# Retention heads: VectorE places all blocks of k, ScalarE all blocks of v

## The chip, the cores and the metric

The kernel runs on one core of one Trainium2 chip. The time is device microseconds (us) of that core, the median of the runs shown. One further execution was profiled, and all rows come from that one.

## The reference, cut to what matters

One step of a two-layer trunk over 320 tokens: 256 of a prompt, 64 of a second group that continues a stored state. Layer 0 projects its input once, to 8 retention heads and a pooling mixer. Layer 1 is an mLSTM mixer. A gated feed-forward block follows each. The change touches the retention heads alone:

```
q, k = rotary(q, pos), rotary(k, pos) * 128 ** -0.5
s      = (q . k) * decay                      # l x m, causal
intra  = s . v                                # sum over tokens m
inter  = (q . S) * q_decay                    # the stored state, second group only
S_new  = gamma ** L * S + (k * k_decay)^T . v  # sum over tokens
ret    = head_rms(intra + inter) * silu(gate)
```

The projections come out with features on the partitions. Both sums over tokens need k and v with tokens on the partitions, so each head turns two arrays of 128 features x 320 tokens.

## The kernel before, in words

**Weights.** All weight matrices are cut into 768 units of 128 x 1024 numbers and pass through a ring of four slots. SyncE (SP) loads a unit (`load`, its issue is L394). ScalarE (ACT) rounds it into `w_hi` (`split`, L909). VectorE (DVE) subtracts to get `w_lo` (`split`, L1323). TensorE (PE) multiplies it (`unit`, L560, 24 matmuls in the retention stage). ScalarE may split unit u only when TensorE has used unit u-4 to the end (it waits for `unit_used` at u-3), and SP may load unit u only when VectorE has split unit u-4. TensorE waits for `lo_ready` before each unit.

**Heads.** A head takes eight units, j = 0 to 7. The first four make q and k in two banks of PSUM, the last four v and the gate. Work that belongs to a head but not to its projection is written out by hand at fixed places j in the next head's units, separately on each engine; each engine takes its own list in order. Head 0's tail and head 1's projection lie in a part of their own ahead of the loop (units 8 to 15). The loops `Fori(0, HEADS - 2)` do the projections of heads 2 to 7 beside the tails of heads 1 to 6. The tail of head 7 runs beside the pooling units.

**Order on VectorE,** for projection h+1 beside tail h, each time after the split of that place: j=0 v and gate scaled by `rt` (L1431, L1432) and v turned by 32 x 32 blocks (L1434, `v_turned`); j=1 half of v placed (L1439); j=2 gate (L1443); j=3 states copied out (L1448, L1449); j=4 rotary on q and k (L1380 to L1389); j=5 k weighted and turned (L1416, L1418, `k_turned`) and half of k placed (L1425); j=6 normalise (L1455, L1456, L1458); j=7 the low part of the result (L1462) and the scores weighted by decay (L1408 to L1411, `ret_intra`). In the part of head 0 the order differs: v of head 0 is turned at j=1, k of head 0 placed at j=1, v of head 0 placed and its scores weighted at j=2, and k of head 1 is turned at j=5 and placed at j=6.

**Order on ScalarE:** j=1 half of v placed (L934) and then the tanh of the gate with its table load (L927); j=4 two copies out of PSUM (L947, L948); j=5 square root (L952); j=6 half of k placed (L942); j=7 high part of the result (L958). In the part of head 0, k is placed at j=1 and v at j=2.

**What "placing" is.** A turn by 32 x 32 blocks leaves each block turned but in its old place. Placing moves block (s, f) from partitions 32f to partitions 32s. One instruction does one pair (s, f) for all token tiles: 32 partitions by 96 for s = 0, 1 and by 64 for s = 2, 3. An array has 16 of them. Before, ScalarE does s = 0, 2 and VectorE s = 1, 3 of both arrays.

**TensorE.** `ret_sums` (L636) stands after the unit of j = 2 of the next head (in the part of head 0, after j = 4). It waits for all four placing semaphores, for `ret_intra` and for the state's load (`ret_s0_loaded`). The units behind it are queued behind that wait. SP issues the state's load (L446) after the store of the previous head's states, behind the eighth load of a head.

Of the kernel before, what the change touches and what calls it, by code (L numbers as in the profile page):

```python
# [10 lines left out]
ACT = mybir.ActivationFunctionType  # L11
# [130 lines left out]
def trunk_kernel(nc, x_in, weights, w_pool_in, cols_in, consts_in, ret_tables_in, ret_state_in, ml_state_in,  # L142
                 y_out, ret_out, pool_out, c_out, m_out, conv_out, ffn_out, m_scratch):
    with ExitStack() as ctx:
# [3 lines left out]
        def sem(name):  # L148
            return ctx.enter_context(nc.semaphore(name))
# [16 lines left out]
        def piece(width, restart=False):  # L166
            if restart:
                used[0] = 0
            at = used[0]
            used[0] += width  # L170
            assert used[0] <= WORK, used
            return work[:, at:at + width]
# [14 lines left out]
        k_tok, v_tok = piece(3 * P), piece(3 * P)  # L187
# [60 lines left out]
        def token_blocks(at):  # L248

            return work[:, at:at + 3 * P].rearrange("p (n s a) -> p n s a", n=3, s=4)  # L250

        k_blocks, v_blocks = token_blocks(k_blocks_at), token_blocks(v_blocks_at)

        def turned_block(turned, s, f):

            return turned[f * 32:(f + 1) * 32, 0:3 - s // 2, s, :]

        def token_rows(tok, s, f):

            return tok.rearrange("p (n c) -> p n c", n=3)[s * 32:(s + 1) * 32, 0:3 - s // 2, f * 32:(f + 1) * 32]  # L260
# [51 lines left out]
        def bank(b, m):  # L312
            return gb[:, 2 * b + m, 0:T]
# [15 lines left out]
        def sems(text):  # L329
            return [sem(name) for name in text.split()]  # L330
# [15 lines left out]
            "first_squares first_sum last_added last_squares z_ready rt_half")  # L346
        dve_step, = sems("dve_step")

        qk_raw, qk_ready, ret_intra, v_tok_ready, ret_state, mix_ready = sems(
            "qk_raw qk_ready ret_intra v_tok_ready ret_state mix_ready")  # L350
        ret_scores, ret_summed, ret_sq_sum = sems("ret_scores ret_summed ret_sq_sum")
        v_turned, v_tok_act, k_turned, k_tok_ready, k_tok_act, gate_ready = sems(
            "v_turned v_tok_act k_turned k_tok_ready k_tok_act gate_ready")
        gate_tanh, ret_sq, ret_std, mix_hi = sems("gate_tanh ret_sq ret_std mix_hi")
        b_ready, = sems("b_ready")
        pooled_ready, pool_summed, pool_hi = sems("pooled_ready pool_summed pool_hi")
# [191 lines left out]
        def _(pe):  # L548
# [86 lines left out]
            def small(out, lhs, rhs, start=True, stop=True):  # L635
                return nc.tensor.matmul(out, lhs, rhs, start=start, stop=stop)  # L636
# [18 lines left out]
                small(ab[:, 2, SEQ + P:SC], k_pad[:, SEQ:3 * P], q_t[:, SEQ:T]).then_inc(ret_scores, 1)  # L655

            def ret_sums(h):
                pe.wait_ge(v_tok_ready, h + 1)
                pe.wait_ge(v_tok_act, h + 1)
                pe.wait_ge(k_tok_ready, h + 1)  # L660
                pe.wait_ge(k_tok_act, h + 1)
                pe.wait_ge(ret_intra, h + 1)
                pe.wait_ge(ret_s0_loaded, h * 16 + 16)
                small(ab[:, 3, 0:SEQ], v_tok[:, 0:P], s_t[:, 0:SEQ], stop=False)
                small(ab[:, 3, P:SEQ], v_tok[:, P:2 * P], s_t[:, SEQ:SEQ + P], start=False)
                small(ab[:, 3, SEQ:T], v_tok[:, 2 * P:3 * P], s_t[:, SEQ + P:SC], stop=False)
                small(ab[:, 3, SEQ:T], ret_s0, q_dec, start=False)
                small(ab[:, 0, 0:P], k_tok[:, 0:P], v_tok[:, 0:P], stop=False)
                small(ab[:, 0, 0:P], k_tok[:, P:2 * P], v_tok[:, P:2 * P], start=False)
                small(ab[:, 0, P:2 * P], k_tok[:, 2 * P:3 * P], v_tok[:, 2 * P:3 * P])\  # L670
                    .then_inc(ret_summed, 1)
# [81 lines left out]
            for p in range(POOL_GROUPS):  # L753
                for kg in range(4):
                    j = 4 * p + kg
# [133 lines left out]
            for m in range(2):  # L889
# [5 lines left out]
                last = small(ab[:, 0, 0:T], ones, sq_last[:, m * T:(m + 1) * T], start=False, stop=m == 1)  # L895
# [4 lines left out]
        def _(act):  # L900
            def split(u):

                if not u.exists:
                    return
                act.wait_ge(raw_loaded[u.slot], u.turn(16, 16))
                if u.i is not None or u.first >= RING:
                    act.wait_ge(unit_used, u.number(1 - RING))
                at = u.slot * UW
                nc.scalar.activation(w_hi[:, at:at + UW], raw[:, at:at + UW], ACT.Copy).then_inc(hi_ready, 1)  # L909
# [19 lines left out]
            def ret_place_v(h):  # L929

                act.wait_ge(v_turned, h + 1)
                for s in (0, 2):
                    for f in range(4):
                        last = nc.scalar.activation(token_rows(v_tok, s, f), turned_block(v_blocks, s, f), ACT.Copy)  # L934
                last.then_inc(v_tok_act, 1)

            def ret_place_k(h):

                act.wait_ge(k_turned, h + 1)
                for s in (0, 2):  # L940
                    for f in range(4):
                        last = nc.scalar.activation(token_rows(k_tok, s, f), turned_block(k_blocks, s, f), ACT.Copy)  # L942
                last.then_inc(k_tok_act, 1)

            def ret_squares(h):
                act.wait_ge(ret_summed, h + 1)
# [56 lines left out]
            for j in range(8):  # L1003
                split(Unit(8 + AHEAD + j))
                if j == 0:
                    act.wait_ge(con_loaded, 16)
                    norm(0)
                if j == 1:
                    ret_place_k(0)
                if j == 2:  # L1010
                    ret_place_v(0)
                    ret_gate(0)
                if j == 5:
                    ret_squares(0)
                if j == 6:
                    ret_std_of(0)
                    ret_place_k(1)
                if j == 7:
                    ret_mix(0)
            with act.Fori(0, HEADS - 2) as i:  # L1020
                for j in range(8):
                    split(Unit(16 + AHEAD + j, i, 8))
                    ret_tail(i + 1, j)
                    if j == 6:
                        ret_place_k(i + 2)
            for j in range(16):
                split(Unit(U_POOL + AHEAD + j))
                ret_tail(HEADS - 1, j)
# [276 lines left out]
        def _(dve):  # L1305
            step = Count(dve_step)
            V = nc.vector
# [31 lines left out]
            def used(u_last):  # L1339

                dve.wait_ge(unit_used, u_last)
# [78 lines left out]
            def ret_place_k(h):  # L1420

                dve.wait_ge(k_turned, h + 1)
                for s in (1, 3):
                    for f in range(4):
                        last = V.tensor_copy(token_rows(k_tok, s, f), turned_block(k_blocks, s, f))  # L1425
                last.then_inc(k_tok_ready, 1)

            def ret_tail(h, j, stored=True):
                if j == 0:
                    used(h * 8 + 8)  # L1430
                    V.tensor_tensor(v_t, bank(1, 0), rt[:], ALU.mult)  # L1431
                    V.tensor_tensor(z_g, bank(1, 1), rt[:], ALU.mult).then_inc(pair_taken, 1)  # L1432
                    dve.wait_ge(pair_taken, h * 2 + 2)
                    V.transpose(o_rs, v_t).then_inc(v_turned, 1)  # L1434
                if j == 1:
                    dve.wait_ge(v_turned, h + 1)
                    for s in (1, 3):
                        for f in range(4):
                            last = V.tensor_copy(token_rows(v_tok, s, f), turned_block(v_blocks, s, f))  # L1439
                    last.then_inc(v_tok_ready, 1)  # L1440
                if j == 2:
                    dve.wait_ge(gate_tanh, h + 1)
                    V.scalar_tensor_tensor(gate, tanh_g, 1.0, z_g, ALU.add, ALU.mult).then_inc(gate_ready, 1)  # L1443
                if j == 3:
                    dve.wait_ge(ret_summed, h + 1)
                    if stored:
                        dve.wait_ge(ret_stored, h * 16)
                    V.tensor_copy(s_new[:, 0:RET_DV], ab[:, 0, 0:P])  # L1448
                    V.scalar_tensor_tensor(s_new[:, RET_DV:2 * RET_DV], ret_s0,  # L1449
                                           con[:, bass.ds(h + CON["gamma_l"], 1)], ab[:, 0, P:2 * P],  # L1450
                                           ALU.mult, ALU.add).then_inc(ret_state, 1)
                if j == 6:
                    dve.wait_ge(gate_ready, h + 1)
                    dve.wait_ge(ret_std, h + 1)
                    step.inc(V.tensor_tensor(mix, mix, gate, ALU.mult))  # L1455
                    step.inc(V.reciprocal(o_rs, o_std))  # L1456
                    own()
                    V.tensor_tensor(mix, mix, o_rs, ALU.mult).then_inc(mix_ready, 1)  # L1458
                if j == 7:
                    dve.wait_ge(mix_ready, h + 1)  # L1460
                    dve.wait_ge(mix_hi, h + 1)
                    V.tensor_tensor(low(b, h), mix, high(b, h).bitcast(F32), ALU.subtract)\  # L1462
                        .then_inc(b_ready, 1)
# [857 lines left out]
```

## Time and profile before

| | us |
|---|---|
| median of 3 runs (2769.45 to 2769.46) | 2769.45 |
| the profiled execution | 2768.36 |
| its span | 2766.5 |
| PE busy | 2745.8 (99%) |
| PEld busy | 2495.7 (90%) |
| DVE busy | 1949.3 (70%) |
| ACT busy | 1453.2 (53%) |

The span is the part that the profile covers; the execution's own time is 1.86 us longer. PE is TensorE's matmuls, PEld its weight loads, which overlap the matmuls. The busy shares are of the span. The clock granted to TensorE was 0.999 of full over the run.

### The profile page before, as it was taken

To read this page: it belongs to the slowest core of one execution; us is meant where nothing else is said; L and a number is where in the kernel's file an instruction comes from. 1 tells how busy PE (TensorE), PEld (TensorE's weight loads), DVE (VectorE), ACT (ScalarE), POOL (GpSimd) and SP (SyncE) were. 2 spreads that over 40 slices of the span, in tenths; PEclk is the share of its full clock that TensorE was granted. 3 is DMA by queue.
4 is the path that set the end of the run, shared out by engine and by line. 5 is a ranking of instruction groups with operands and counts; after the bars stand their busy time and mean duration, and the time that the engine had idled before them with its cause. 6 is when DMAs were issued, how large, how long until landed. Compare 5 with 4: busy or idle time off the path is not lost.

```text
span 2766.5 us, 44056 instructions
## 1 busy us (share of the span) xinstructions
PE 2745.8 (99%) x15341; PEld 2495.7 (90%) x15341; DVE 1949.3 (70%) x3202; ACT 1453.2 (53%) x2441; POOL 160.3 (6%) x134
## 2 busy tenths in 40 slices
PE   9999999999999999999999999999999999999998
PEld 8999988888888888888999999888888888888887
DVE  8877677676567665668887778667675667655776
ACT  6555345665345543555555566546654455535554
POOL 0000032000000000002300000330000000000004
PEclk9999999999999999999999999999999999999999
DMA  6444345454545454544444444444444444444443
GB/s 241 153 154 152 125 137 165 143 165 140 167 142 164 143 165 141 165 143 148 161 149 147 153 147 154 140 146 152 157 148 160 146 159 148 155 160 147 152 149 128
DMA packets 120999, 422.64 MB, mean 153 GB/s; under 512 B 13704, under 2 KB 18320, under 8 KB 120720
## 3 DMA queue, kind: packets, MB, share of 16 engines
q1 hardware_dynamic: 120704, 420.41, 46.3%
q8 instruction: 120, 1.97, 0.3%
q14 instruction: 31, 0.25, 0.0%
q10 hardware_dynamic: 144, 0.01, 0.0%
HBM read 414.22 MB, written 6.14 MB: 152 GB/s over the span
## 4 chain that ended last, share of the span: by engine, by line
PE 94%; DVE 3%; ACT 1%; issue 1%; DMA 1%; SPq 0%; DVEq 0%; ACTq 0%
PE gb L600 38%; PE gb L610 25%; PE gb L560 18%; PE ab L570 10%; PE ab L636 3%; DVE w_lo L1323 1%; ACT w_hi L909 1%; DMA raw<-in_weights 1%; ACT work L1039 0%; DVE rt L1336 0%; DVE work L1494 0%; DVE work L2160 0%; DVE work L1892 0%; DVE work L1547 0%; ACT work L999 0%
## 5 line engine op out<-in xcount | busy, mean ns | idle before, releaser
L1323 DVE TENSOR_TENSOR w_lo<-raw,w_hi 128x1024 fp32r<-128x1024 f32 x766 | 951.2, 1254 | 512.2 <-ACT w_hi L909 507.2
L909 ACT ACTIVATE w_hi<-raw 128x1024 fp32r<-128x1024 f32 x768 | 809.0, 1058 | 873.1 <-PE gb L610 416.0
L600 PE MATMUL gb<-a,w_hi 128*128 128x512 f32 x2816 | 684.0, 390 | 0.0
L560 PE MATMUL gb<-a,w_hi 128*128 128x320 f32 x2784 | 619.4, 311 | 3.6 <-DVE a L1330 2.1
L600 PEld LDWEIGHTS gb<-a,w_hi 128*128 128x128 f32 x2816 | 525.0, 188 | 105.4
L560 PEld LDWEIGHTS gb<-a,w_hi 128*128 128x128 f32 x2784 | 464.8, 188 | 6.4 <-DVE a L1330 2.4
L600 PE MATMUL gb<-b,w_hi 128*128 128x512 f32 x1920 | 464.8, 390 | 0.0
L560 PE MATMUL gb<-a,w_lo 128*128 128x320 f32 x1392 | 430.2, 309 | 0.0
L610 PE MATMUL gb<-a,w_lo 128*128 128x320 f32 x2816 | 426.9, 309 | 0.0
L610 PEld LDWEIGHTS gb<-a,w_lo 128*128 128x128 f32 x2816 | 419.8, 188 | 6.8
L600 PEld LDWEIGHTS gb<-b,w_hi 128*128 128x128 f32 x1920 | 358.0, 188 | 71.8
L1039 ACT ACTIVATE work<-work 32x128 f32<-32x128 f32 x960 | 295.7, 308 | 206.5 <-DVE work L1347 195.7
L610 PE MATMUL gb<-b,w_lo 128*128 128x320 f32 x1920 | 292.5, 309 | 0.0
L610 PEld LDWEIGHTS gb<-b,w_lo 128*128 128x128 f32 x1920 | 286.8, 188 | 5.4
L560 PEld LDWEIGHTS gb<-a,w_lo 128*128 128x128 f32 x1392 | 261.3, 188 | 0.0
L520 POOL TENSOR_TENSOR sq_one<-x 128x320 f32 x60 | 69.8, 1163 | 2573.1 <-DVE x L1371 2562.5
L570 PE MATMUL ab<-w_hi,a 128*128 128x512 f32 x704 | 188.6, 390 | 0.6 <-ACT w_hi L909 0.6
L570 PEld LDWEIGHTS ab<-w_hi,a 128*128 128x128 f32 x704 | 131.8, 188 | 29.0 <-ACT w_hi L909 1.9
L570 PE MATMUL ab<-w_hi,b 128*128 128x512 f32 x480 | 128.8, 390 | 0.2 <-ACT w_hi L909 0.2
L570 PEld LDWEIGHTS ab<-w_hi,b 128*128 128x128 f32 x480 | 89.5, 188 | 19.3 <-DVE b L1715 0.7
L1659 DVE TENSOR_TENSOR work<-gb,rt 128x384 f32<-128x384 f32 x44 | 24.6, 559 | 105.0 <-PE gb L600 105.0
L1369 DVE TENSOR_TENSOR x<-gb,x 128x640 f32 (+1 forms) x63 | 52.0, 825 | 64.5 <-PE gb L600 53.1
(216 smaller groups left out, 1662.9 us busy)
## 6 DMA issues: line engine op xcount, KB each, us to landing
raw<-in_weights SPq DMA_DIRECT2D x768, 512.0 KB, 3.4
work<-in_ret_tables SPq DMA_DIRECT2D x8, 320.0 KB, 3.7
out_c<-work SPq DMA_DIRECT2D x8, 257.0 KB, 5.1
x<-in_x SPq DMA_DIRECT2D x3, 640.0 KB, 8.9
work<-m_scratch SPq DMA_DIRECT2D x8, 192.0 KB, 4.8
out_y<-work SPq DMA_DIRECT2D x3, 480.0 KB, 3.5
work<-in_ml_state SPq DMA_DIRECT2D x8, 128.5 KB, 4.7
raw<-in_weights SPq DMA_DIRECT2D x4, 256.0 KB, 4.9
```

The costliest lines, as they stand in the source:

```text
L520: step.inc(nc.gpsimd.tensor_tensor(sq_one[:], tile(x, t), tile(x, t), ALU.mult))
L560: last = nc.tensor.matmul(bank(b, m), w[:, at:at + P], v, start=kg == k == n == 0, stop=kg == groups - 1 and k == UK - 1 and n == 2)
L570: last = nc.tensor.matmul(out, act[:, t:t + P], w[:, :, k, :], start=q == k == 0, stop=q == quads - 1 and k == UK - 1)
L600: last = nc.tensor.matmul(gb[:, 2 * p + m, :], w_hi[:, at:at + P], act[:, t:t + 512], start=q == k == 0, stop=final and low_first and k == ...
L610: last = nc.tensor.matmul(bank(p, m), w_lo[:, at:at + P], act[:, t:t + T], start=False, stop=final and not low_first and k == UK - 1)
L636: return nc.tensor.matmul(out, lhs, rhs, start=start, stop=stop)
L909: nc.scalar.activation(w_hi[:, at:at + UW], raw[:, at:at + UW], ACT.Copy).then_inc(hi_ready, 1)
L1039: last = nc.scalar.activation(left_t_blocks[feats * 32:(feats + 1) * 32, :, tokens, :], left_blocks[tokens * 32:(tokens + 1) * 32, :, feat ...
L1323: V.tensor_tensor(w_lo[:, at:at + UW], raw[:, at:at + UW], w_hi[:, at:at + UW].bitcast(F32), ALU.subtract).then_inc(lo_ready, 1)
L1369: step.inc(V.tensor_tensor(two(tiles(x, p * 2)), banks(b), two(tiles(x, p * 2)), ALU.add))
L1659: V.tensor_tensor(two(low_gate)[:, :, 0:WIDE_LO], lows_of(0), r[:, :, 0:WIDE_LO], ALU.mult)
```

## The change

The numbers of instructions, their shapes and their sources stay; who issues them and when changes. VectorE's `ret_place_k` now does all four s, 16 copies where it did 8; ScalarE's is gone. ScalarE's `ret_place_v` does all four s, 16 copies where it did 8; VectorE's placing of v at j = 1 is gone. The semaphores `v_tok_ready` and `k_tok_act` go, and with them two of TensorE's waits.

```diff
             def ret_sums(h):
-                pe.wait_ge(v_tok_ready, h + 1)
                 pe.wait_ge(v_tok_act, h + 1)
                 pe.wait_ge(k_tok_ready, h + 1)
-                pe.wait_ge(k_tok_act, h + 1)
                 pe.wait_ge(ret_intra, h + 1)
...
             def ret_place_v(h):      # ScalarE
                 act.wait_ge(v_turned, h + 1)
-                for s in (0, 2):
+                for s in range(4):
                     for f in range(4):
                         last = nc.scalar.activation(token_rows(v_tok, s, f), turned_block(v_blocks, s, f), ACT.Copy)
                 last.then_inc(v_tok_act, 1)
-
-            def ret_place_k(h):
-
-                act.wait_ge(k_turned, h + 1)
-                for s in (0, 2):
-                    for f in range(4):
-                        last = nc.scalar.activation(token_rows(k_tok, s, f), turned_block(k_blocks, s, f), ACT.Copy)
-                last.then_inc(k_tok_act, 1)
...
-                if j == 1:
-                    ret_place_k(0)
...
                     ret_std_of(0)
-                    ret_place_k(1)
...
                     ret_tail(i + 1, j)
-                    if j == 6:
-                        ret_place_k(i + 2)
...
             def ret_place_k(h):      # VectorE
                 dve.wait_ge(k_turned, h + 1)
-                for s in (1, 3):
+                for s in range(4):
                     for f in range(4):
                         last = V.tensor_copy(token_rows(k_tok, s, f), turned_block(k_blocks, s, f))
                 last.then_inc(k_tok_ready, 1)
...
-                if j == 1:
-                    dve.wait_ge(v_turned, h + 1)
-                    for s in (1, 3):
-                        for f in range(4):
-                            last = V.tensor_copy(token_rows(v_tok, s, f), turned_block(v_blocks, s, f))
-                    last.then_inc(v_tok_ready, 1)
```

## Rows read from the trace of the kernel before

**Rows 1.** The page: busy time and share of each engine; chain that ended last.

```profile
PE 2745.8 (99%) x15341; PEld 2495.7 (90%) x15341; DVE 1949.3 (70%) x3202; ACT 1453.2 (53%) x2441; POOL 160.3 (6%) x134
...
PE 94%; DVE 3%; ACT 1%; issue 1%; DMA 1%; SPq 0%; DVEq 0%; ACTq 0%
```

**Rows 2.** Waits of PE: releaser, us in total, times, longest.

```profile
PE ab L636 <- DVE b L1462: 0.6, 1, 0.6
...
PE ab L636 <- DVE work L1411: 0.4, 1, 0.4
```

**Rows 3.** Timeline of DVE, head 0: start, duration (both us), line, count.

```profile
50.91 0.51 DVE L1434 STREAM_TRANSPOSE work<-work 128x320 f32<-128x320 f32 x1
51.45 1.71 DVE L1425 COPY work<-work 32x96 f32<-32x96 f32 x8
...
56.87 0.21 DVE L1411 TENSOR_TENSOR work<-work 128x64 f32<-128x64 f32 x1
57.20 1.23 DVE L1323 TENSOR_TENSOR w_lo<-raw,w_hi 128x1024 fp32r<-128x1024 f32 x1
```

**Rows 4.** Timeline of ACT, head 0, the second placing and what follows.

```profile
52.22 2.21 ACT L934 ACTIVATE work<-work 32x96 f32<-32x96 f32 x8
...
56.12 1.05 ACT L909 ACTIVATE w_hi<-raw 128x1024 fp32r<-128x1024 f32 x1
```

**Rows 5.** Timeline of PEld (weight loads), the sums of head 0.

```profile
57.30 0.84 PEld L636 LDWEIGHTS ab<-work 128*128 128x128 f32 x5 [0.64 <-issue]
```

**Rows 6.** Timeline of DVE, from k of head 1 to v of head 1.

```profile
67.61 1.72 DVE L1425 COPY work<-work 32x96 f32<-32x96 f32 x8
...
71.94 0.49 DVE L1458 TENSOR_TENSOR work<-work 128x320 f32<-128x320 f32 x1
...
76.74 0.51 DVE L1434 STREAM_TRANSPOSE work<-work 128x320 f32<-128x320 f32 x1
```

**Rows 7.** Timeline of ACT beside it.

```profile
72.47 0.47 ACT L958 ACTIVATE b<-work 128x320 fp32r<-128x320 f32 x1 [2.65 <-DVE work L1458]
...
77.28 2.22 ACT L934 ACTIVATE work<-work 32x96 f32<-32x96 f32 x8 [1.34 <-DVE work L1434]
...
81.19 1.99 ACT L909 ACTIVATE w_hi<-raw 128x1024 fp32r<-128x1024 f32 x2
87.21 1.06 ACT L909 ACTIVATE w_hi<-raw 128x1024 fp32r<-128x1024 f32 x1 [4.03 <-PE gb L560]
```

**Rows 8.** Timeline of PE, the sums of head 1.

```profile
81.72 0.59 PE L636 MATMUL ab<-work 128*128 128x256 f32 x2
```

**Rows 9.** Timeline of SPq, the state's load for head 1; its time to landing.

```profile
78.00 0.34 SPq L446 DMA_DIRECT2D work<-in_ret_state  x1
...
DMA to landing us min/median/max: 3.2/3.2/3.2
```

**Rows 10.** Timeline of DVE in the loop, up to v of head 3.

```profile
132.51 0.49 DVE L1458 TENSOR_TENSOR work<-work 128x320 f32<-128x320 f32 x1
...
135.26 1.22 DVE L1323 TENSOR_TENSOR w_lo<-raw,w_hi 128x1024 fp32r<-128x1024 f32 x1
...
137.31 0.51 DVE L1434 STREAM_TRANSPOSE work<-work 128x320 f32<-128x320 f32 x1
```

**Rows 11.** Timeline of ACT in the loop, the same head.

```profile
133.13 0.47 ACT L958 ACTIVATE b<-work 128x320 f32 x1 [2.42 <-DVE work L1458]
134.05 1.06 ACT L909 ACTIVATE w_hi<-raw 128x1024 fp32r<-128x1024 f32 x1 [0.45 <-PE gb L560]
137.57 1.06 ACT L909 ACTIVATE w_hi<-raw 128x1024 fp32r<-128x1024 f32 x1 [2.46 <-PE gb L560]
138.54 2.21 ACT L934 ACTIVATE work<-work 32x96 f32<-32x96 f32 x8
```

**Rows 12.** Timeline of PEld and of PE, the sums of head 3.

```profile
144.27 0.88 PEld L636 LDWEIGHTS ab<-work 128*128 128x128 f32 x5
...
144.41 0.81 PE L636 MATMUL ab<-work 128*128 128x256 f32 x4
```

More of the change, by code:

```diff
@@ L347, in trunk_kernel @@
         dve_step, = sems("dve_step")
-        qk_raw, qk_ready, ret_intra, v_tok_ready, ret_state, mix_ready = sems(
-            "qk_raw qk_ready ret_intra v_tok_ready ret_state mix_ready")
+        qk_raw, qk_ready, ret_intra, ret_state, mix_ready = sems(
+            "qk_raw qk_ready ret_intra ret_state mix_ready")
         ret_scores, ret_summed, ret_sq_sum = sems("ret_scores ret_summed ret_sq_sum")
-        v_turned, v_tok_act, k_turned, k_tok_ready, k_tok_act, gate_ready = sems(
-            "v_turned v_tok_act k_turned k_tok_ready k_tok_act gate_ready")
+        v_turned, v_tok_act, k_turned, k_tok_ready, gate_ready = sems(
+            "v_turned v_tok_act k_turned k_tok_ready gate_ready")
         gate_tanh, ret_sq, ret_std, mix_hi = sems("gate_tanh ret_sq ret_std mix_hi")
```

## The prediction, made before the changed kernel was run

> **What bounds the kernel now.** I read the page's busy shares and chain first: TensorE is busy for 99% of the span and makes 94% of the chain that ended last [rows 1]. No engine beside it can make the kernel faster by more than the little that TensorE stands idle; any stall of TensorE that the change adds is paid in full, unless a later wait takes it back. So the second view is who TensorE waits for. Two entries touch the retention heads: 0.4 us for the decay weighting of head 0 (L1411) and 0.6 us for the last low part of the heads, L1462 [rows 2]. No placing releases it anywhere. The third view is therefore the timeline around `ret_sums`, engine by engine: how long before TensorE arrives are k and v in place? I did this for head 0, head 1 and a head of the loop, since the three have different neighbours.
>
> **What the change is, in instructions.** Per array and head, eight copies on VectorE last 1.71 to 1.72 us [rows 3, 6], eight on ScalarE 2.21 to 2.22 [rows 4, 7, 11]. In all VectorE loses and gains 64 copies, ScalarE too, so total busy time hardly moves. What moves is place. On VectorE, 1.72 us goes from behind v's turn to ahead of it. On ScalarE, 2.2 us that lay beside VectorE's half now stands in line behind it: v is placed 4.43 us after its turn (2.21 for the first eight, 2.22 from start to start for the second), where it took ScalarE 2.21 and VectorE about as long.
>
> **Head 0.** v's turn starts at 50.91 and lasts 0.51 [rows 3]. ScalarE, now without k, starts at 51.45 and ends 4.43 later, at 55.88. VectorE places k from 51.45 to 54.92, then splits and weights; it did 8 + split + 8 before and does 16 + split now, so L1411 still starts at 56.87 and ends at 57.08 [rows 3]. TensorE's weight load came at 57.30, 0.22 later [rows 5]. v is ready 1.2 us before that: cost 0, and the 0.4 us wait stays as well. But ScalarE's tanh and splits follow its placing. The split of unit 14 started 1.69 after eight copies had ended (54.43 to 56.12 [rows 4]); now it starts at 55.88 + 1.69 = 57.57, lasts 1.06, and VectorE, which waits for it, starts its own at 58.66 instead of 57.20 [rows 3]. VectorE runs on without a gap from there to k of head 1, so everything up to 67.61 [rows 6] comes 1.46 late. Nothing that TensorE needs in this stretch is late.
>
> **Head 1.** k of head 1 costs VectorE 1.72 more at j = 6, and it stays without a gap: 1.46 + 1.72 = 3.18 late. v's turn, 76.74 before [rows 6], starts at 79.92 and ends at 80.43. ScalarE starts as before 0.03 later (77.25 to 77.28 [rows 6, 7]), at 80.46; its high part and two splits come in time, since its row at 72.47 moves with L1458 [rows 6, 7] to 75.65 and two splits of about 1 us follow. It ends at 80.46 + 4.43 = 84.89. TensorE is there much earlier: the sums' first matmul was at 81.72 [rows 8], its weight load 0.14 ahead as in the loop [rows 12], at 81.58. With the 0.22 from release to weight load it starts at 85.11. **Stall: 85.11 - 81.58 = 3.5 us.** All units of TensorE behind `ret_sums` wait with it. For the price of passing a release, the bounds are 0.03 (VectorE to ScalarE, rows 6 and 7) and 0.22 (rows 3 and 5): I take the second, which is TensorE's own. Both ends give 3.3 to 3.5.
>
> **Is it given back?** The lateness of ScalarE and VectorE against TensorE goes at the next place where they wait for it: ScalarE stood idle for 4.03 us before its split at 87.21 [rows 7]. After the change the pair of splits ahead of it starts at 84.89 + 1.69 = 86.58 instead of 81.19, and TensorE has moved by 3.5, so against TensorE ScalarE is 1.9 later, within those 4.03. TensorE itself has no gap in the heads that it could shorten. The 0.6 us for L1462 [rows 2] comes from work on VectorE that starts at a unit's end, so it travels with TensorE and stays.
>
> **Heads 2 to 7,** all alike, by head 3. VectorE comes to the loop's k as before, since both helpers have caught up. Sixteen copies make it 1.72 late; v's turn moves from 137.31 [rows 10] to 139.03 and ends at 139.54. ScalarE's high part moves from 133.13 with L1458 [rows 10, 11] to 134.85 and its next split (at most 0.45 later, as it waited before) to 135.3, done at 136.4; VectorE needs it at 135.26 + 1.72 = 136.98 [rows 10]. The split at 137.57 [rows 11] stays, so ScalarE is free at 138.6, starts at 139.57 and ends at 144.00. TensorE's weight load stands at 144.27 [rows 12]. Ready at 144.03 to 144.22, by the two bounds: a slack of 0.05 to 0.24 us, where ScalarE's half had 3.5 to spare. Cost 0, but barely, six times; if the estimate is wrong by 0.2 us, each head pays about 0.1.
>
> **Transfers.** The loads of weights wait for VectorE's splits, which come up to 3.2 us late once; ScalarE's splits are later still. The state of head 1 matters more: its issue at 78.00 stands behind the load released by such a split. 78.00 + 3.18 + 3.2 to landing [rows 9] = 84.4, half a microsecond ahead of v. Hidden, and late next if v were faster. The waits removed from TensorE cost nothing that the trace shows.
>
> **The page against the row.** ScalarE's eight copies take 2.21 us, 0.28 each, beginning to end, no overlap between neighbours [rows 4, 11]. The Trainium skill, page "ScalarE: Activation LUTs", section "What ACT_TABLE_LOAD costs", gives an ACTIVATE with immediate scale 186 ns + 0.833 ns per element and says that back-to-back ones overlap by about 93 ns. By that sixteen would take an estimated 8 x 0.173 + 8 x 0.146 = 2.55 us; head 0 would then make nothing late, v of head 1 would be there at 77.28 + 1.72 + 2.55 + 0.22 = 81.8, the state's load at 82.9 would be last, and the stall 1.3 us. The trace disagrees with the page for these 32-partition copies, and decides.
>
> **The sum.** 2768.36 of the profiled execution + 3.5 = 2771.9. The median of the runs is 1.09 higher than that execution, so 2769.45 + 3.5 = 2772.95, some 0.13% slower. What a measurement of this kernel can tell from no change is about 0.2%, 5.5 us: by that bound the forecast is "same", with a sign.
>
> **Rivals.**
> 1. *Every head stalls.* The slack of 0.05 to 0.24 in the loop is gone because a copy for s = 1, 3 is dearer on ScalarE, or because ScalarE's high part, now close to its loop's end, delays the split and with it v's turn. For: six heads with almost no slack. Against: the shapes are the same, and the split has 0.6 us of its own slack. Price: 3.5 + 6 x (0.1 to 0.5) = 4.1 to 6.5, say 2774.2. Beyond 0.2% only where a head loses 0.34 or more. Chance 0.14.
> 2. *Not slower.* v of head 1 comes in time, because VectorE isn't late: it would need ScalarE's split of unit 14 to come in time and the second half of v to be placed within 1.1 us of v's turn; or the wait for L1411 falls, worth 0.4. It decides from where v's turn of head 1 ends before 81.58 - 0.22 - 4.43 = 76.9, which is even earlier than the 77.25 of now. So a stall of 0.3 comes with no lateness at all. Price: -0.4 to +0.3, 2769.4. Chance 0.08.
> 3. *The state's load is last.* If it is stretched by the weights' loads beside it, by 1 us, it lands at 85.4 and the stall is 4.2: 2773.6. Chance 0.08.
> 4. *Sixteen copies cost ScalarE less than twice eight,* because neighbours overlap in a longer run. The nearest faster rows are VectorE's own, 2 x 1.72 = 3.44 [rows 6]. Then v of head 0 ends at 54.89, VectorE is 0.47 late and not 1.46, v of head 1 is turned at 79.44 and ready at 79.47 + 3.44 + 0.22 = 83.1; the state's load at 78.00 + 2.19 + 3.2 = 83.4 is last. Price 1.8: 2771.3. Against: the eight show no sign of it. Chance 0.06. The page named above is this rival's, with a still smaller stall.
>
> The forecast has 0.64. **Range:** it takes in rivals 3 and 4 and most of 1, and the release bounds: 2770.5 to 2775.6. Slower by over 0.2% is the far part of rival 1 and what I don't see, 0.07. Faster by over 0.2% would need 5.5 us out of TensorE's idle time, of which two named waits of the heads make 1.0 us: 0.02. Within 0.2%: 0.91.
>
> **What would show it.** Right: a new entry among TensorE's waits, L636 released by ScalarE's placing (L934 of now), once, 3.4 to 3.6 us long, near 81.7; L934 in runs of 16 lasting 4.4 us; v's turn of head 1 near 79.9; ScalarE's idle time for k gone; the sums of the loop's heads 31.3 us apart with gaps under 0.1. Wrong: no gap at 81.7, or the releaser is a DMA, or six gaps of equal size. The forecast is wrong as a whole if the span grows by less than 2 us or more than 5.

## The result, and the profile after

| | kernel before | changed kernel |
|---|---|---|
| median of 9 runs, us | 2769.38 (2768.57 to 2769.93) | 2777.71 (2774.62 to 2780.66) |
| profiled execution, us | 2768.36 | 2780.66 |
| its span, us | 2766.5 | 2778.9 |

The ratio is 1.0031 (95% interval 1.0022 to 1.0039): the change costs 8.3 us. Forecast were 3.5 us, a time of 2773.0 and a range up to 2775.6. The direction was right; the size was not, and the result lies outside the range. The changed kernel also scatters over 6 us where the kernel before scatters over 1.4, and its profiled execution is the slowest of the nine. What is read from its trace explains 12.4 us of span, more than the median lost. Line numbers have moved: in the changed kernel L932 is ScalarE's placing of v, L907 its split and L925 the tanh; L1308 is VectorE's split, L1403 the turn of k, L1410 its placing and L1419 the turn of v.

The page, the lines that answer to [rows 1]: busy time of each engine, and the chain that ended last.

```profile
PE 2749.6 (99%) x15341; PEld 2498.0 (90%) x15341; DVE 1947.5 (70%) x3202; ACT 1452.8 (52%) x2441; POOL 160.2 (6%) x134
...
PE 87%; DVE 6%; ACT 3%; DMA 2%; issue 1%; SPq 0%; DVEq 0%; ACTq 0%
```

Busy times hardly move, as forecast. But the chain leaves TensorE far more often, and it now has a share of DMA twice as large. The waits of PE (us in total, times, longest), which answer to [rows 2]:

```profile
PE ab L636 <- ACT work L932: 9.5, 7, 3.2
```

One such entry was forecast, once, 3.4 to 3.6 us long. It is there seven times. (The longest is 3.2 us by the matmuls and 3.51 us by the weight loads, which were to start first; from here on gaps are those of the weight loads.) Where in the heads it stands is seen in the timeline of PEld, the weight loads with which `ret_sums` begins (start, duration, and in brackets the gap before and its releaser). They answer to [rows 5, 8, 12]; shown are heads 0, 1, 2 and 7, and the gaps of heads 3 to 6 are 1.48, 1.45, 1.33 and 1.21:

```profile
58.26 1.85 PEld L636 LDWEIGHTS ab<-work 128*128 128x128 f32 x14 [0.35 <-issue]
...
86.08 1.85 PEld L636 LDWEIGHTS ab<-work 128*128 128x128 f32 x14 [3.51 <-ACT work L932]
...
118.59 1.85 PEld L636 LDWEIGHTS ab<-work 128*128 128x128 f32 x14 [1.17 <-ACT work L932]
...
281.99 1.85 PEld L636 LDWEIGHTS ab<-work 128*128 128x128 f32 x14 [1.17 <-ACT work L932]
```

The sums of head 1 in the kernel before, which had no gap:

```profile
81.57 1.89 PEld L636 LDWEIGHTS ab<-work 128*128 128x128 f32 x14
```

From there to the sums of head 3 at 144.27 [rows 12] are 62.70 us: before, the sums of the loop's heads stood 31.35 us apart. From 86.08 to 281.99 are 195.91 us, against 6 x 31.35 = 188.10: the six heads of the loop lose 7.81. The account of the 12.4 us:

- up to the sums of head 0: 58.26 - 57.30 [rows 5] = 0.96. This isn't put down to the change. At 41 us, ahead of the first placed block, TensorE is already 1.25 us late (42.42 against 41.17); in the nine traces of the experiments it is 0.2 to 1.2 us late there. The granted clock averages 0.66 between 15 and 20 us, against 1.00 in the trace of before; but it is 0.66 in the repeat of the changed kernel too (experiment 5), whose sums start at 57.29.
- head 1: 86.08 - 81.57 (before) - 0.96 = 3.55, the stall that was forecast.
- heads 2 to 7: 7.81, forecast at nothing.
- what is left is 0.1: behind the heads the two kernels run alike.

**Who makes the loop's heads late.** The waits of DVE between 40 and 330 us have an entry that the kernel before doesn't have:

```profile
DVE work L1401 <- DMA work<-in_ret_tables: 8.7, 6, 1.6
```

L1401 is the first line of `ret_turn_k`, which multiplies k by the head's decay. It waits for the load of the decay table, once in each of six heads. The timeline of DVE for one of them, from the split ahead of k's turn to the turn of v:

```profile
97.95 1.22 DVE L1308 TENSOR_TENSOR w_lo<-raw,w_hi 128x1024 fp32r<-128x1024 f32 x1
100.50 0.49 DVE L1401 TENSOR_TENSOR work<-work 128x320 f32<-128x320 f32 x1 [1.33 <-DMA work<-in_ret_tables]
...
113.54 0.51 DVE L1419 STREAM_TRANSPOSE work<-work 128x320 f32<-128x320 f32 x1
```

k's turn is 1.33 late by the table, the sixteen copies add their 1.72, and v's turn follows. ScalarE starts on v at 114.09, ends at 118.55, and TensorE starts at 118.59, 1.17 late.

**Why the table is late.** SP issues it behind the fourth load of the head's weights, and each load of weights waits until VectorE's split has set its buffer free. First the issues of SPq for the table of head 2 in the kernel before (start, duration), and the time of each to landing (last number, in the same order):

```profile
83.66 0.33 SPq L394 DMA_DIRECT2D raw<-in_weights  x1
85.20 0.33 SPq L394 DMA_DIRECT2D raw<-in_weights  x1
89.69 0.33 SPq L394 DMA_DIRECT2D raw<-in_weights  x1
90.22 0.33 SPq L441 DMA_DIRECT2D work<-in_ret_tables  x1
```
```profile
raw<-in_weights SPq DMA_DIRECT2D x1, 512.0 KB, 3.3
raw<-in_weights SPq DMA_DIRECT2D x1, 512.0 KB, 4.0
raw<-in_weights SPq DMA_DIRECT2D x1, 512.0 KB, 3.4
work<-in_ret_tables SPq DMA_DIRECT2D x1, 320.0 KB, 3.6
```

The same for the changed kernel:

```profile
90.19 0.33 SPq L394 DMA_DIRECT2D raw<-in_weights  x1
91.73 0.33 SPq L394 DMA_DIRECT2D raw<-in_weights  x1
94.16 0.33 SPq L394 DMA_DIRECT2D raw<-in_weights  x1
94.68 0.33 SPq L441 DMA_DIRECT2D work<-in_ret_tables  x1
```
```profile
raw<-in_weights SPq DMA_DIRECT2D x1, 512.0 KB, 3.3
raw<-in_weights SPq DMA_DIRECT2D x1, 512.0 KB, 4.5
raw<-in_weights SPq DMA_DIRECT2D x1, 512.0 KB, 5.5
work<-in_ret_tables SPq DMA_DIRECT2D x1, 320.0 KB, 5.8
```

The first two loads are released 6.5 us later than before, the third and the table only 4.5 later. What was spread over 6.6 us is now issued within 4.5. The table lands 5.8 us after its issue, at 100.5, which is where L1401 starts. The cause of the late release is ScalarE's timeline:

```profile
81.58 4.45 ACT L932 ACTIVATE work<-work 32x96 f32<-32x96 f32 x16 [2.44 <-DVE work L1419]
86.04 1.28 ACT L925 ACT_TABLE_LOAD   x1
87.34 0.47 ACT L925 ACTIVATE work<-work 128x320 f32<-128x320 f32 x1
87.72 1.99 ACT L907 ACTIVATE w_hi<-raw 128x1024 fp32r<-128x1024 f32 x2
```

Its next two splits stand behind sixteen copies, a table load and the tanh, so they start at 87.72 instead of 81.19 [rows 7]. VectorE's splits and SP's loads follow them. TensorE, meanwhile, has only moved by 4.5.

### The profile page after: what moved, and what is told of

It reads as the page before. It is cut to its first block, busy times and chain, and to the rows that moved or that the text cites. A ratio compares the mean times of both kernels' runs of the same rounds, so it can differ in the third digit from the quotient of the medians.

```text
span 2778.9 us, 44042 instructions
## 1 busy us (share of the span) xinstructions
PE 2749.6 (99%) x15341; PEld 2498.0 (90%) x15341; DVE 1947.5 (70%) x3202; ACT 1452.8 (52%) x2441; POOL 160.2 (6%) x134
## 4 chain that ended last, share of the span: by engine, by line
PE 87%; DVE 6%; ACT 3%; DMA 2%; issue 1%; SPq 0%; DVEq 0%; ACTq 0%
PE gb L600 38%; PE gb L610 24%; PE gb L560 13%; PE ab L570 10%; PE ab L636 2%; DVE w_lo L1308 2%; DMA work<-in_ret_tables 1%; ACT work L932 1%; ACT w_hi L907 1%; DVE work L1410 1%; DVE work L1435 1%; ACT work L1024 0%; DMA raw<-in_weights 0%; DVE rt L1321 0%; DVE work L1419 0%
## 5 line engine op out<-in xcount | busy, mean ns | idle before, releaser
L1308 DVE TENSOR_TENSOR w_lo<-raw,w_hi 128x1024 fp32r<-128x1024 f32 x766 | 950.5, 1253 | 516.3 <-ACT w_hi L907 511.5
L907 ACT ACTIVATE w_hi<-raw 128x1024 fp32r<-128x1024 f32 x768 | 807.8, 1058 | 849.1 <-PE gb L610 416.0
```

The costliest lines, as they stand in the source:

```text
L1308: V.tensor_tensor(w_lo[:, at:at + UW], raw[:, at:at + UW], w_hi[:, at:at + UW].bitcast(F32), ALU.subtract).then_inc(lo_ready, 1)
```

## The experiments

All were timed in five rounds beside runs of the kernel before on the same chip. The ratios are to that kernel.

**1. The table's load early.** The changed kernel, with the decay table issued behind the first load of weights instead of the fourth.

```diff
-                for j in range(4):
-                    load(Unit(8 + j, h, 8))
+                load(Unit(8, h, 8))
                 sp.wait_ge(ret_intra, h)
                 sp.dma_start(ret_table, head_row(ret_tables_in, h)).then_inc(ret_table_loaded, 16)
-                for j in range(4, 8):
+                for j in range(1, 8):
                     load(Unit(8 + j, h, 8))
```

> The changed kernel, with the load of a head's decay table issued by SP behind the first of the head's eight weight loads and not behind the fourth. Theory (table): in heads 2 to 7 VectorE waits for this table before it can weight and turn k, because ScalarE's long placing of v makes the two weight loads ahead of it late, so that three loads and the table go out within 4.5 us and the table lands in 5.8 instead of 3.6. Then the table is there in time, VectorE's wait for it goes, the six stalls of 1.2 to 1.5 us fall to 0.1 or less, and only head 1's 3.5 stays: 2769.4 + 3.5 = 2772.9, with less spread from run to run than the changed kernel (2774.6 to 2780.7). Rival (copies): v placed by ScalarE alone is too slow in every head whatever the table does; six stalls stay near 1.3 and the time near 2777.7.

Measured: 2773.98 (2773.19 to 2775.15, 11 runs) against 2769.07 (2768.36 to 2770.70, 33 runs), ratio 1.0019 (1.0010 to 1.0028). VectorE doesn't wait for the table any more. PEld's timeline, the sums of heads 1, 2 and 7:

```profile
85.18 3.35 PEld L635 LDWEIGHTS ab<-work 128*128 128x128 f32 x14 [3.54 <-ACT work L931]
...
118.14 1.89 PEld L635 LDWEIGHTS ab<-work 128*128 128x128 f32 x14
...
274.87 1.89 PEld L635 LDWEIGHTS ab<-work 128*128 128x128 f32 x14
```

Head 1's stall is as it was; from head 2 to head 7 are 156.73 us, which is 5 x 31.35 to within 0.02, and no gap is left. So the table's late landing is needed for the loop's stalls, and the slack of 0.05 to 0.24 us that was forecast without it is enough. Measured it is 0.24: ScalarE's copies for head 3 end at 149.24, and the weight load starts at 149.48. The run is 1.1 us above the expectation, and one reason is in the first row: fourteen loads in 3.35 us where they took 1.85, and 32.96 us to the next sums instead of 31.35. The window just behind the stall in this kernel (the stretch; its length; busy time of PE, PEld, DVE, ACT and POOL; the granted clock; DMA share; GB/s):

```profile
86.00:87.00 1.00, 1.00 (x6) 0.94 (x5) 0.00 (x0) 0.99 (x3) 0.00 (x0) 0.50 0.01 5
```

In the stall the granted clock was 1.00. Behind it TensorE runs at 0.50, its 1.2 GHz level, and between 88.5 and 90.0 us the mean is back at 0.91. That makes the stall dearer by 32.96 - 31.35 = 1.6 us.

**2. Half of the change: ScalarE all of v,** k in halves as before. The edit is to the kernel before; VectorE's placing of v is gone.

```diff
             def ret_place_v(h):
...
-                for s in (0, 2):
+                for s in range(4):
```

> Half of the change: ScalarE places all of v, k stays half on each engine. Theory (table): ScalarE's splits behind the long placing are as late as in the changed kernel, so VectorE still waits 1.3 to 1.6 us for the table in heads 2 to 7, but VectorE has not the 1.7 us of further copies, v's turn is only about 1.5 late and the sums of heads 2 to 7 stall by 0.3 or less. Head 0: ScalarE places k, then all of v, its split of unit 14 starts at 58.3 instead of 56.1, VectorE is 2.2 late; the weighting comes early, so the old 0.4 us wait of head 0 goes. Head 1: v ready at 84.2 against 81.2, stall 3.0, net +2.6: 2772.0. Rival (copies): the loop's six heads stall by over 1 us here too, 2779.

Measured: 2774.23 (2771.97 to 2777.47, 11 runs), ratio 1.0020 (1.0011 to 1.0029). The forecast of six waits for the table was a miss:

```profile
DVE work L1415 <- DMA work<-in_ret_tables: 1.6, 2, 1.1
```
```profile
85.27 1.85 PEld L636 LDWEIGHTS ab<-work 128*128 128x128 f32 x14 [3.42 <-ACT work L933]
...
116.57 1.89 PEld L636 LDWEIGHTS ab<-work 128*128 128x128 f32 x14
```

The table comes late twice, and then on time: its median landing is 4.0 us, against 5.9 in the changed kernel. The two waits are for head 1, 0.48 us, and for head 2, 1.12. The first is part of head 1's gap, which was forecast at 3.0 and is 3.42. 31.30 us lie between the sums of heads 1 and 2, so the second cost nothing: VectorE, which has only eight copies of k, has 1.7 us more in hand. Moving v alone makes the stall of head 1 but not those of the loop. Its profiled span is 2771.3, 4.8 over that of before, and up to the last sums it had lost 3.65. The other 1.1 us come far behind the heads, in layer 1: two gaps of the weight loads, 0.41 us before 1572.19 and 0.59 before 1666.01, and among the waits of PE an entry that the kernel before doesn't have, for VectorE's L1897 (0.5 us, 2 times). Why VectorE is late there no run shows.

**3. The other half: VectorE all of k,** v in halves. ScalarE's placing of k is gone, as in the changed kernel.

```diff
             def ret_place_k(h):
...
-                for s in (1, 3):
+                for s in range(4):
```

> The other half of the change: VectorE places all of k, v stays half on each engine. Theory (table): ScalarE's splits are on time, the table lands in 3.6 to 3.7 us and VectorE does not wait for it; the loop's six heads have no stall, since v's second half is done by VectorE at 142.4 of 144.3. Head 0 pays: 16 copies of k and 8 of v stand ahead of the weighting, which is 1.7 late: stall 1.7 more. Head 1: VectorE 3.4 late, last copies ready at 83.8 against 83.3: 0.5. Sum +2.2: 2771.6. Rival (copies): no stall in the loop either, so only the table rows tell.

Measured: 2772.61 (2770.67 to 2773.15, 11 runs), ratio 1.0012 (1.0002 to 1.0021). Head 0's weighting is late by VectorE's longer line, as expected: 

```profile
60.10 2.56 PEld L636 LDWEIGHTS ab<-work 128*128 128x128 f32 x14 [2.22 <-issue]
...
86.24 1.85 PEld L636 LDWEIGHTS ab<-work 128*128 128x128 f32 x14 [0.26 <-issue]
```
```profile
62.00:63.00 1.00, 1.00 (x6) 1.00 (x6) 0.55 (x2) 0.01 (x1) 0.00 (x0) 0.50 0.77 225
```

The gap of 2.22 is 1.6 over the 0.64 of before, forecast 1.7. The window shows a granted clock of 0.50 here too, behind the gap. From these sums to the next are 26.14 us, against 24.27 before, of which 0.26 is a gap: the other 1.6 is the clock, more than the 1.0 us that the median lies over the 2771.6 expected. The loop has no stall and no wait for the table. By experiments 2 and 3, neither half makes the loop stall; only both together do.

**4. The table early, and ScalarE's split of unit 14 ahead of placing v of head 0.**

```diff
             for j in range(8):
-                split(Unit(8 + AHEAD + j))
+                if j != 3:
+                    split(Unit(8 + AHEAD + j))
...
                 if j == 2:
+                    split(Unit(8 + AHEAD + 3))
                     ret_place_v(0)
```

> As the table moved forward, and in the part of head 0 ScalarE splits unit 14 ahead of placing v of head 0 instead of behind the tanh. My account of head 1's 3.5 us is 1.5 of lateness from that split, 1.7 from the eight further copies of k and 0.3 from the second half of v. If it holds, the stall of head 1 falls to 2.0 and the time to 2769.4 + 2.0 = 2771.4. Rival: the state's load of head 1, half a microsecond behind v, is what ends the wait; it comes 1.5 earlier too, so then also about 2.0, but released by a DMA. If the split has no part in it, 3.5 stays and the time is as with the table moved alone.

Measured: 2770.84 (2770.10 to 2773.04, 11 runs), ratio 1.0007 (0.9998 to 1.0016).

```profile
83.62 1.85 PEld L635 LDWEIGHTS ab<-work 128*128 128x128 f32 x14 [1.98 <-ACT work L931]
```

The 1.46 us by which the prediction held VectorE late out of head 0 are worth 3.54 - 1.98 = 1.56 of head 1's stall. The medians of experiments 1 and 4 differ by more, 3.1 us: here the clock doesn't fall behind the stall (31.31 us to the next sums), and in experiment 1's trace that cost 1.6. What is left is 2770.84 - 2769.07 = 1.8 us of the change's 8.3, with an interval that takes in no change, though each engine still places a whole array.

**5. The changed kernel once more,** for its scatter.

> The changed kernel itself once more, on the chip of these runs, for a second profile and for its spread. The table account: the loop's six stalls come with a table that lands in 4.5 to 6 us behind two or three weight loads that are still in flight; landings differ from run to run, so the six stalls differ, between 0.3 and 1.5 us each, and the time spreads over some 6 us (2774.6 to 2780.7 so far) where the kernel before spreads over 2. Rival (copies): the stalls are set by the engines' instruction times, which repeat to 0.1 us, and would be alike in both profiles; the spread is then without a cause in the heads.

Measured: 2778.76 (2778.49 to 2781.29, 5 runs) against 2769.19 (2768.60 to 2770.23, 22 runs), ratio 1.0037 (1.0023 to 1.0051). In this profiled execution (2780.41) the same code loses its time elsewhere:

```profile
86.12 3.49 PEld L636 LDWEIGHTS ab<-work 128*128 128x128 f32 x14 [4.53 <-ACT work L932]
...
119.83 1.89 PEld L636 LDWEIGHTS ab<-work 128*128 128x128 f32 x14
...
152.09 1.85 PEld L636 LDWEIGHTS ab<-work 128*128 128x128 f32 x14 [0.87 <-ACT work L932]
```
```profile
68.20 0.49 DVE L1401 TENSOR_TENSOR work<-work 128x320 f32<-128x320 f32 x1 [1.03 <-DMA work<-in_ret_tables]
```

Here the table of head 1 is late already, and lengthens that stall by its 1.03. The clock falls to 0.50 behind it, and head 2 has no gap. The six gaps of the loop are 0, 0.87, 1.43, 1.48, 0.56 and 0.75, where they were 1.17 to 1.48 in the first trace. Head 2 has none because TensorE's slow stretch gives the loads time: the third goes out at 96.60, 4.84 behind the second, and the table lands in 3.7. From head 0's sums to head 7's this trace takes 224.42 us and the first 223.73, against 212.35 before: nearly the same loss, split in two ways.

The gaps follow the landings. In the two traces and that of experiment 6, fifteen heads of the loop have a gap, and in all fifteen it is the time that the head's table took to land, 5.2 to 6.1 us, less 4.6, within 0.03. The three heads without a gap have landings of 3.7, 3.8 and 4.3. So each tenth of a microsecond of landing beyond 4.6 costs TensorE a tenth, and the landings, which differ from head to head and run to run, can spread the time as seen.

**6. The split of unit 14 moved, the table left where the change has it.**

```diff
             for j in range(8):
-                split(Unit(8 + AHEAD + j))
+                if j != 3:
+                    split(Unit(8 + AHEAD + j))
...
                 if j == 2:
+                    split(Unit(8 + AHEAD + 3))
                     ret_place_v(0)
```

> The changed kernel with ScalarE's split of unit 14 moved ahead of placing v of head 0, and the decay table's load left in its place. The two causes add: head 1's stall falls from 3.5 to 2.0 us as it did with the table moved, and the loop's six stalls stay, since they don't come from head 1: 1.5 below the changed kernel, about 2776. Rival: the stalls of the loop are an echo of head 1's stall, passed on from head to head, and fall with it: 2771 to 2773.

Measured: 2778.50 (2778.28 to 2778.66, 6 runs), ratio 1.0034 (1.0022 to 1.0046): no gain, a miss.

```profile
67.18 0.49 DVE L1403 TENSOR_TENSOR work<-work 128x320 f32<-128x320 f32 x1 [1.58 <-DMA work<-in_ret_tables]
```
```profile
85.13 2.97 PEld L636 LDWEIGHTS ab<-work 128*128 128x128 f32 x14 [3.59 <-ACT work L932]
```

VectorE comes 1.5 us earlier to the turn of head 1's k and waits 1.58 for that head's table, which is issued at 60.86, 0.52 behind a load, and takes 6.2 to land. In the kernel before, this table had landed only 0.2 us ahead of its user (60.65 + 4.6 = 65.2, and L1416 starts at 65.43). The late split and the late table lie side by side; one of them alone removed gives back nothing at head 1 (3.54 in experiment 1, 3.59 here), and only together are they worth 1.6 (experiment 4). The rival, that the loop's stalls are an echo of head 1's, isn't tested by this, since head 1's stall didn't fall; experiments 1 and 8 rule it out, with head 1's stall and none in the loop.

**7. The arrays swapped,** as an edit to the kernel before: ScalarE places all of k, which comes early, VectorE all of v. The other engine's placing of each array is gone. ScalarE's split of unit 13 stands ahead of the placing of k of head 0.

```diff
             def ret_place_k(h):      # ScalarE
...
                 act.wait_ge(k_turned, h + 1)
-                for s in (0, 2):
+                for s in range(4):
...
             for j in range(8):
-                split(Unit(8 + AHEAD + j))
+                if j != 2:
+                    split(Unit(8 + AHEAD + j))
...
                 if j == 1:
+                    split(Unit(8 + AHEAD + 2))
                     ret_place_k(0)
...
                 if j == 1:           # VectorE
                     dve.wait_ge(v_turned, h + 1)
-                    for s in (1, 3):
+                    for s in range(4):
```

> The other way round: ScalarE places all of k (16 copies, 4.4 us) and VectorE all of v (16 copies, 3.4 us); in the part of head 0 ScalarE splits unit 13 ahead of placing k. v is the array placed last before the sums, and now the faster engine has it, with nothing added ahead of v's turn; ScalarE's long placing lies at j = 6, where it has waited for TensorE. Head 0: split 13 and 16 copies of v end at 56.15, the weighting is as before. Head 1: last copy at 81.5, needed at 81.58 less 0.2: stall 0 to 0.2. Loop: v done at 143.4 of 144.3, the table lands in 3.7 as before. Sum 0 to +0.3: 2769.1 to 2769.4. Rival (all of one array on one engine costs, whichever way): 2773 or more.

Measured: 2768.60 (2767.78 to 2769.46, 11 runs) against 2769.19, ratio 0.9998 (0.9989 to 1.0007).

```profile
PE ab L636 <- DVE work L1421: 0.3, 1, 0.3
```
```profile
DVE work L1406 <- DMA work<-in_ret_tables: 1.0, 1, 1.0
```

With the same number of copies on each engine the loss is gone. So it isn't that one engine places an array alone, but which array each engine has. The split of unit 13 was moved with it, and no run here parts the two.

**8. ScalarE's tanh one unit later in the loop,** the table left in place. It moves the release of the loads without touching the placing or the table.

```diff
                 if j == 1:
                     ret_place_v(h)
+                if j == 2:
                     ret_gate(h)
```

> The changed kernel with ScalarE's tanh of the gate, and its table load, one place later in the loop (behind the split of j = 2 and not ahead of it); the decay table stays in its place in SP's list. The split of j = 2 starts 1.7 us earlier, so the weight load that it releases goes out earlier and the three loads ahead of the decay table are less bunched. Table account: the table lands sooner than 5.8 us, VectorE's wait for it shrinks and with it the six stalls, from 1.3 to between 0 and 0.7; head 1's 3.5 stays: 2773 to 2777. Rival (copies): nothing changes ahead of v's placing, so the stalls stay and the time with them.

Measured: 2774.17 (2772.74 to 2775.82, 11 runs), ratio 1.0019 (1.0010 to 1.0028). No wait for the table, and no stall in the loop: the sums of heads 2 to 7 stand 31.35 apart. ScalarE in head 2, its split now straight behind the copies and ahead of the tanh:

```profile
113.68 4.50 ACT L932 ACTIVATE work<-work 32x96 f32<-32x96 f32 x16 [0.93 <-DVE work L1420]
118.20 1.06 ACT L907 ACTIVATE w_hi<-raw 128x1024 fp32r<-128x1024 f32 x1
119.28 1.28 ACT L925 ACT_TABLE_LOAD   x1
```

The stalls were forecast at 0 to 0.7 us and the time at 2773 to 2777; both came. The loads behind it and the table are issued at 120.69, 123.43, 126.51 and 127.03, over 6.3 us, and land in 3.4, 3.2, 3.4 and 3.6 us. In the changed kernel the same four are issued at 122.70, 124.24, 126.68 and 127.20, over 4.5 us, and land in 3.2, 4.5, 5.8 and 6.1. The issue and the landing of the table, here and then in the changed kernel:

```profile
127.03 0.33 SPq L441 DMA_DIRECT2D work<-in_ret_tables  x1
work<-in_ret_tables SPq DMA_DIRECT2D x1, 320.0 KB, 3.6
```
```profile
127.20 0.33 SPq L441 DMA_DIRECT2D work<-in_ret_tables  x1
work<-in_ret_tables SPq DMA_DIRECT2D x1, 320.0 KB, 6.1
```

The table is issued at the same place in SP's order and at nearly the same time; only the loads ahead of it are spread. That settles the cause: the table is late because the loads bunch, and the loads bunch because ScalarE's splits stand behind the placing and the tanh.

**9. The swap of experiment 7, with the table early** as in experiment 1.

> The swapped placing (k by ScalarE, v by VectorE) with the decay table's load behind the first of a head's weight loads. In the swapped kernel's profile VectorE waited 1.0 us for head 1's table and TensorE 0.3 us for the last copy of v of head 1. Table account: the first wait goes and the second with it; nothing else in the heads stalls but the decay weighting of head 0 and L1462's place. 0.3 less than the swapped kernel at the same start: 2768.3, no more than 0.8 under the kernel before, so within what can be told from no change. Rival: the wait of 0.3 comes from ScalarE's 16 copies of k ahead of its split at j = 7, which also holds VectorE; the table moved alone then changes nothing: 2768.6.

Measured: 2768.56 (2767.91 to 2768.98, 11 runs) against 2769.01 (2768.21 to 2769.63, 14 runs), ratio 0.9998 (0.9989 to 1.0008).

```profile
81.68 1.89 PEld L635 LDWEIGHTS ab<-work 128*128 128x128 f32 x14
```

Head 1's wait for v is gone, and VectorE's for the table, as by the table account. The time doesn't part it from its rival (2768.3 and 2768.6 were expected). Both medians of the swap lie about 0.5 us under the kernel before, within what can't be told from it. No kernel here beats it for certain.

## Why the prediction was wrong, by its own steps

- **What bounds the kernel.** Right: the stalls of the heads were paid in full (12.3 of the 12.4 us of span were lost by the last sums), and no busy time mattered.
- **Head 0.** Right that it costs nothing, wrong in a detail. The sixteen copies of ScalarE took 4.46, and no placing releases TensorE. That the 0.4 us wait for the weighting stays was wrong: it is gone from the waits of PE, and the gap ahead of the sums falls from 0.64 [rows 5] to 0.35. That gains 0.3 us, which a start of the sums at 57.34 in experiment 1, against 57.30, hides, since TensorE is 0.34 late there at 41 us already. For the lateness, experiment 4 gives back 1.56 for the 1.46 us late out of this head.
- **Head 1.** Right in the first profile and not in each execution. Forecast 3.5; found 3.51, and 3.54 with the table early. The table of head 1 can lengthen it (4.53 in the repeat), and the clock behind it can add 1.6.
- **Is it given back?** Right for the span: nothing came back. Wrong in what it looked at. It found ScalarE 1.9 us later against TensorE within 4.03 us of idle time, which came true (1.96 of idle time are left ahead of that split), and stopped there, because the next split could take it. It didn't ask what those late splits release.
- **Heads 2 to 7, "Cost 0, but barely".** This step failed: forecast 0, found 7.8 us in the first profile. Its premise was that VectorE comes to the loop's k as before "since both helpers have caught up". They had caught up with their splits, but k's turn was late by the table, 1.33 us in head 2. The arithmetic behind the premise was good: with the table on time (experiments 1 and 8) the slack held six times out of six.
- **Transfers.** This is where the failure began. The step said that the loads come late and followed one load behind them, the state's. The decay table stands behind four loads in SP's order, its issue and its user are both in the kernel's text and in the trace of before, and it was never looked at. In that trace it lands at 90.22 + 3.6 = 93.8, and k's turn came 0.8 us later, by VectorE's timeline of before:

```profile
94.63 0.48 DVE L1416 TENSOR_TENSOR work<-work 128x320 f32<-128x320 f32 x1
```

  That is little enough to be listed as the next to be late; for head 1's table it was 0.2 (experiment 6). The prediction also took landing times as fixed (3.2 for the state). The table's went from 3.6 to 5.8 when the loads ahead of it closed up.
- **The page against the row.** The Trainium skill, page "ScalarE: Activation LUTs", section "What ACT_TABLE_LOAD costs", would have made sixteen copies an estimated 2.55 us. The traces disagree: they take 4.44 to 4.50 us in them, twice the 2.21 or 2.22 of eight [rows 4, 7].
- **Rivals.** Rival 1 (every head stalls, 0.14) named the right place and the right weakness, the six thin slacks, but neither the cause nor the price: it gave 0.1 to 0.5 us a head, and the first profile shows 1.17 to 1.48. Rival 3 looked for a late load and picked the wrong one. Rivals 2 and 4 didn't occur.
- **The signs.** "Six gaps of equal size" was listed as a sign of being wrong, and so was a span that grows by more than 5; the gaps came, 1.17 to 1.48, and the span grew by 12.4.
- **The range** ended at 2775.6 because every late term was priced as an error of the copies. A thin slack six times over, with a load behind it whose landing isn't fixed, should have had an upper end of six stalls of a microsecond.

**What stays open.** What in a stall decides whether the clock falls behind it (below). Why VectorE is late for TensorE twice in layer 1 in experiment 2. And the split of the median's 8.3 us: by experiment 1's median against the changed kernel's, in different calls, some 3.7 hang on the table (2777.71 - 2773.98) and 4.9 on head 1 with its clock; the profiled executions, the slow end of the runs, put 7.8 and 3.6. No profile of one of the quicker executions was taken.

## What to carry to other kernels

When a change makes an engine late, follow what it sets free and not only what it feeds: each buffer it releases late is a load issued late, closer to the next ones, and the load to worry about is the unrelated one queued behind them. List every load in the queue's order with its landing and its user, and its slack, before pricing anything at nothing. And give long work that nobody waits for (a tanh with its table load) a place behind the work that releases loads: moving one call was worth as much as moving the load.

## What the runs showed of the hardware that was not expected

**A stall of TensorE can cost more than its length.** In stretches behind stalls the granted clock falls from 1.00 to 0.50 (2.4 to 1.2 GHz). It fell behind gaps of 2.22 (experiment 3), 3.54 (1), 3.59 (6 and 8) and 4.53 us (5). It didn't behind 1.98 (4), 3.42 (2) and 3.51 us (the changed kernel's first trace). Each trace also has a gap of TensorE near 15 us, where it waits for VectorE: the clock fell to 0.50 behind 2.06 to 2.39 us in seven of the eleven traces, and not behind 1.62 (6), 2.02 (1), 2.12 (before) and 2.59 us (9). Length alone doesn't sort these: 2.06 fell and 3.51 didn't. The price in the heads, by the distance to the next sums over 31.35, was 1.5 to 1.6 us in experiments 1, 6 and 8 and 119.83 - 86.12 - 31.35 = 2.4 us in experiment 5.

**The landing of a load depends on how close its neighbours are.** These are SyncE's loads of the loop, in the trace of before and the first of the changed kernel. 512 KB land in 3.2 to 3.7 us when the issue before lies 4 us or more back. With 1.5 us they land in 4.0 to 4.8, and as the third within 4.0 us in 5.5 to 5.8. The 320 KB of the table, always 0.52 us behind a load, land in 3.6 to 3.9 behind a spread row and in 5.8 to 6.1 behind a bunched one. It isn't a fixed price: in experiment 6 one row bunched in the same way landed in 4.1 and its table in 4.3, and that head has no stall.
